# Second attention of a two-block fp32 model: matmuls over the full 128x128 array, other gates, other placing of the projection steps

## The reference

```python
kband, vband = with_prev(kb), with_prev(vb)      # block of 128 tokens and the one before it
s_band = einsum('bnqkgd,bnskd->bnkgqs', qb, kband) * scale + bias_band   # masked to the band
s_meta = einsum('bnqkgd,bmkd->bnkgqm', qb, k_meta) * scale + bias_m      # 16 meta keys
p = softmax(concatenate([s_meta, s_band, sink], -1), -1)
out = einsum(p_meta, v_meta) + einsum(p_band, vband)
y_att = att @ w_attn_branch
merged = sigmoid(g_ssd + gb[0]) * y_ssd + sigmoid(g_att + gb[1]) * y_att
h = h + merged @ w_out
```

## Time and profile before

| | us |
|---|---|
| time, median of 3 runs | 2701.64 (2695.93 to 2713.91) |
| the profiled execution, time | 2691.95 |
| its span, first to last instruction | 2690.0 |
| PE busy in the span | 2522.0 (94%) |
| DVE busy | 1632.3 (61%) |
| ACT busy | 899.1 (33%) |
| mean granted TensorE clock of the span | 0.965 |

### The profile page before, as it was taken

The page is one execution under the profiler, slowest core; times in us unless marked ns, Lnnn a source line. Parts: engine busy times, 40 slices in busy tenths (PEclk is TensorE's granted clock), DMA queues, the critical chain, the costliest instruction groups (busy, mean ns, idle before and its releaser), DMA issues.

```text
span 2690.0 us, 40344 instructions
## 1 busy us (share of the span) xinstructions
PE 2522.0 (94%) x15581; PEld 2210.7 (82%) x15581; DVE 1632.3 (61%) x2776; ACT 899.1 (33%) x1341; POOL 62.2 (2%) x55
## 2 busy tenths in 40 slices
PE   6999999998988999999989899889998999999997
PEld 4887888876887987888888788879777789999997
DVE  6556444456387845444587687877554555884684
ACT  3122222234354532222336634652232233222222
POOL 0000000000021000000000000001000000000000
PEclk9999999999988999999999999989998999999998
DMA  4235222334441012222225223412111112223222
GB/s 139 94 102 124 94 94 94 135 118 121 137 114 41 24 63 83 94 94 94 94 80 126 80 71 108 112 58 90 45 54 50 56 63 95 78 88 117 93 94 95
DMA packets 89708, 242.46 MB, mean 90 GB/s; under 512 B 24870, under 2 KB 56102, under 8 KB 65574
## 3 DMA queue, kind: packets, MB, share of 16 engines
q1 hardware_dynamic: 29056, 198.26, 20.7%
q10 hardware_dynamic: 58744, 36.42, 6.2%
q0 software_dynamic: 1760, 5.77, 1.0%
HBM read 230.50 MB, written 11.14 MB: 90 GB/s over the span
## 4 chain that ended last, share of the span: by engine, by line
PE 48%; DVE 8%; issue 3%; ACT 2%; ACTq 0%; DVEq 0%
PE ps L1151 26%; PE ps L927 13%; PE ps L1239 3%; DVE wlo L1389 1%; PE ps L1327 1%; PE ps L1294 1%; ACT L L776 1%; PE ps L1329 1%; PE ps L1330 1%; PE ps L1310 1%; PE ps L1313 0%; PE ps L1293 0%; ACT whi L506 0%; PE ps L1202 0%; PE ps L1204 0%
## 5 line engine op out<-in xcount | busy, mean ns | idle before, releaser
L506 ACT ACTIVATE whi<-raw 128x2048 fp32r<-128x2048 f32 x187 | 357.6, 1912 | 754.3 <-PE ps L927 501.5
L1151 PE MATMUL ps<-parts,whi 128*128 128x264 f32 x2752 | 488.6, 295 | 5.3 <-issue 4.7
L1389 DVE TENSOR_TENSOR wlo<-raw,whi 128x2048 fp32r<-128x2048 f32 x187 | 427.4, 2286 | 66.6 <-ACT whi L506 65.8
L927 PE MATMUL ps<-parts,whi 128*128 128x512 f32 x1360 | 435.0, 401 | 14.7 <-DVE wlo L1389 9.9
L1151 PEld LDWEIGHTS ps<-parts,whi 128*128 128x128 f32 x2752 | 396.2, 193 | 19.4 <-issue 16.7
L927 PEld LDWEIGHTS ps<-parts,whi 128*128 128x128 f32 x1360 | 259.0, 191 | 80.0 <-DVE wlo L1389 9.3
L927 PE MATMUL ps<-parts,wlo 128*128 128x512 f32 x680 | 271.8, 400 | 0.0
L1151 PE MATMUL ps<-parts,wlo 128*128 128x264 f32 x1200 | 247.4, 288 | 0.0
L927 PE MATMUL ps<-Mhi,whi 128*128 128x512 f32 x512 | 203.2, 397 | 5.1 <-DVE Mlo L1480 5.1
L927 PE MATMUL ps<-Mhi,wlo 128*128 128x512 f32 x512 | 203.0, 396 | 0.0
L927 PE MATMUL ps<-Mlo,whi 128*128 128x512 f32 x512 | 203.0, 396 | 0.0
(11 more groups left out here) (355 smaller groups left out, 4050.4 us busy)
## 6 DMA issues: line engine op xcount, KB each, us to landing
raw<-in_stream SPq DMA_DIRECT2D x187, 1024.0 KB, 4.8
csb<-sums_d ACTq DMA_DIRECT2D x16, 512.0 KB, 5.6
bands<-scratch ACTq DMA_DIRECT2D x6, 1024.0 KB
near<-bands ACTq DMA_DIRECT2D x20, 256.0 KB, 2.6
csf<-sums_d ACTq DMA_DIRECT2D x32, 128.0 KB, 6.0
Qst<-parts POOLq DMA_DIRECT2D x14, 256.0 KB, 6.3
tabs<-bands ACTq DMA_DIRECT2D x8, 418.0 KB, 3.0
...
```

Of the source, the lines that this page charges most:

```text
L506: nc.scalar.activation(whi[:, s, :], raw[:, s, :], ACT.Copy).then_inc(hi_done, 1)
L927: mm = nc.tensor.matmul(out, w[:, s, at], x(k), start=k + j == 0, stop=k == k_tiles - 1 and j == 2)
L1151: mm = nc.tensor.matmul(ps[:, 2 * par + h, 0:HALF], w[:, s, at], x[:, k, h * HALF:(h + 1) * HALF], start=k + j == 0, stop=k == k_tiles - 1 ...
L1389: nc.vector.tensor_tensor(wlo[:, s, :], raw[:, s, :], whi[:, s, :].bitcast(F32), ALU.subtract).then_inc(lo_done, 1)
```

## The change

- Scores: a head's keys are kept in `keys2` with zeros in the other head's 64 rows, so `scores(n)` is one matmul over all 128 rows: 273 columns (previous chunk, sink and meta, own chunk; 145 for the first chunk; 34 for both heads' meta queries in step 8). `Pb` and the bias table are laid out in that order, which cuts one of the DMAs that spread the table (early in the program) in two.
- Values: `vals2` has a zero slot beside each chunk's values, so a slice of 128 weight columns puts the result into the head's half of the partitions and zeros into the other. One matmul per block of keys serves up to 256 queries (its own chunk and the next one); the steps alternate between the heads. `Pb` keeps all eight steps' rows.
- Meta keys: their probabilities of all eight steps are gathered on DVE (`meta_columns`), transposed once and used in four matmuls at the end of the pair (`values_meta`).
- Gates: sigmoid(x) becomes (1 + tanh(x/2))/2. The bias goes into the tanh on ACT, the 1 into the multiply on DVE, the factor 1/2 into the addition after `out`.
- k-steps: the first tile of the loop is done ahead of the pairs; then two k-steps stand in front of each attention step (three ahead of the first; one in the last pair of each `i`, which has one tile less).
- `split_low` is cut into two halves, put behind different steps.

The diff, cut to its core (of the pair loop on PE and on DVE the new lines only; the old ones are in the listing above):

```diff
+                keys2 = sb("keys2", [P, 2, QT, ROW1], F32, scope)
+                vals2 = sb("vals2", [P, 2 * QT + 1, DH], F32, scope)
...
+                Pb = sb("Pb", [P, 2 * QT, ROW], F32, scope)
...
-                    spread(bands2[:, :, ROW0:ROW], two + BAND2 + P - 1, P, 2 * P)
+                    spread(bands2[:, :, 0:P], two + BAND2 + P - 1, P, P)
+                    spread(bands2[:, :, P + ROW0:ROW], two + BAND2 + 2 * P - 1, P, P)
...
-                    act.wait_ge(gs_new, i * 4 + (p + 1))
-                    nc.scalar.activation(sq[:, 0, :], sq[:, 0, :], ACT.Sigmoid).then_inc(gs_sig, 1)
-                    for n in range(8):
-                        if n < 7:
-                            exps(n + 2)
-                        if n == 0 and p % 2 == 0:
+                    for n in range(7):
+                        exps(n + 2)
+                        if n == 2 and p % 2 == 0:
                             next_unit("pair", 3 * p // 2, turn=i * 6, half_turn=i * 3)
+                        if n == 3:
+                            act.wait_ge(mt_free, i * 12 + (T0["pair"] + 3 * p + 2))
+                            nc.scalar.activation(sq[:, 0, :], sq[:, 0, :], ACT.Tanh, scale=0.5, bias=gate_h[:, bass.ds(i * 4 + p, 1)]).then_inc(gs_sig, 1)
...
             with pe.Fori(0, 2) as i:
+                def pair_tile(rr, ks):
+                    tile2("pair", rr // 2, rr % 2, H2, ks, turn=i * 6)
+                pair_tile(0, range(KT))
                 for p in range(4):
                     base = i * 40 + 10 * p
+                    steps = [(3 * p + 1 + j, k) for j in range(3 if p < 3 else 2) for k in range(KT)]
+                    def dense(n):
+                        for _ in range(n):
+                            rr, k = steps.pop(0)
+                            pair_tile(rr, range(k, k + 1))
                     def scores(n):
                         if n >= 2:
+                            pe.wait_ge(ttr2, base + (n - 1))
                         if n == 8:
+                            mm = nc.tensor.matmul(ps[:, 4, 0:2 * ROW0], Q2[:, 0:P], keys2[:, :, 0, 0:ROW0], start=True, stop=True)
                         else:
+                            h, c = n % 2, 1 + n // 2
+                            at = CHUNKS[c][0]
+                            row = keys2[:, h, :, :].rearrange("p c n -> p (c n)")
+                            keys = row[:, (c - 2) * ROW1 + ROW0:c * ROW1] if c > 1 else row[:, 0:ROW1]
+                            mm = nc.tensor.matmul(ps[:, 4 + n % 2, 0 if c > 1 else P:ROW], Q2[:, at:at + P], keys, start=True, stop=True)
+                        mm.then_inc(s2_full, 1)
+                    def turn(n):
+                        pe.wait_ge(p2_ready, i * 36 + (9 * p + n + 1))
+                        if n or p:
+                            pe.wait_ge(pt2_dve, base + n)
+                        if n >= 2:
+                            nc.tensor.transpose(ps[:, 6, 0:P], Pb[:, n, 0:P], ident)
+                        nc.tensor.transpose(ps[:, 6, P:2 * P], Pb[:, n, P + ROW0:ROW], ident).then_inc(pt2_full, 1)
...
+                    def values(n):
+                        pe.wait_ge(pt2_dve, base + (n + 1))
+                        h, c = n % 2, 1 + n // 2
+                        if n == 2 and p:
                             pe.wait_ge(at_ready, i * 4 + p)
+                        for block in range(c - 2, c if c == QT else c - 1):
+                            w = 2 * P if block < QT - 1 else P
+                            mm = nc.tensor.matmul(ps[:, 7, block * P:block * P + w], vals2[:, 2 * block + 1 - h:2 * block + 3 - h, :].rearrange("p a d -> p (a d)"),
+                                                  PT2[:, h, 2 * block * P:2 * block * P + w], start=n == 2, stop=False, skip_group_check=True)
+                    def values_meta():
+                        pe.wait_ge(pt2_dve, base + 10)
+                        for c in range(QT):
+                            mm = nc.tensor.matmul(ps[:, 7, c * P:(c + 1) * P], vmeta[:, c, :], PTm[:, :], start=False, stop=c == QT - 1, skip_group_check=True)
+                        mm.then_inc(o2_full, 1)
...
+                    if not p:
+                        pe.wait_ge(kv_staged, i + 1)
+                    dense(2)
+                    pe.wait_ge(mt_free, i * 12 + (T0["pair"] + 3 * p + 1))
                     if p:
+                        pe.wait_ge(first_done, i * 4 + p)
                     scores(0)
                     scores(1)
                     for n in range(8):
+                        dense(3 if not n else 2 if p < 3 else 1)
                         if n < 7:
                             scores(n + 2)
+                        if n >= 3:
                             values(n - 1)
                         turn(n)
+                    dense(1)
+                    turn_first()
                     values(7)
+                    turn_meta()
+                    dense(2)
+                    values_first()
+                    values_meta()
+                    dense(len(steps))
...
+            own.mark(nc.vector.memset(keys2[:, :, :, :], 0.0))
+            own.mark(nc.vector.memset(vals2[:, :, :], 0.0))
...
+                    nc.vector.scalar_tensor_tensor(halves(Q2[:, :]), product_ready(3 * p), DH ** -0.5, halves(R[:, :]), ALU.mult, ALU.mult).then_inc(mt_free, 1)
                     dve.wait_ge(tabs_loaded, i * 128 + 32 * (p + 1))
                     softmax_in(0)
                     softmax_in(1)
+                    if p:
+                        heads_high(p - 1)
                     for n in range(8):
+                        softmax_out(n)
                         if n < 7:
                             softmax_in(n + 2)
+                        else:
+                            meta_columns()
+                            softmax_out(8)
+                        turned(n)
+                        if n == 0 and p:
+                            heads_low(p - 1)
+                        if n in (1, 2) and p % 2:
+                            split_low("pair", 3 * p // 2, i * 6, n - 1)
+                        if n == 3:
+                            nc.vector.tensor_tensor(halves(sq[:, 0, :]), product_ready(3 * p + 1), halves(R[:, :]), ALU.mult).then_inc(mt_free, 1)
+                        if n in (4, 5) and p % 2 == 0:
+                            split_low("pair", 3 * p // 2, i * 6, n - 4)
+                        if n == 6:
                             dve.wait_ge(gs_sig, i * 4 + (p + 1))
+                            y = t_at(YS, i * 4 + p)
+                            nc.vector.scalar_tensor_tensor(y, sq[:, 0, :], 1.0, y, ALU.add, ALU.mult)
+                        if n == 7 and p < 3:
+                            gate_att()
+                    turned_first()
+                    if p == 1:
+                        split_low("pair", 2, i * 6, 0)
+                    turned_meta()
+                    if p == 1:
+                        split_low("pair", 2, i * 6, 1)
+                    first_out()
+                    if p == 3:
+                        gate_att()
+                        split_low("pair", 5, i * 6)
+                heads_high(3)
+                heads_low(3)
...
-                nc.vector.tensor_tensor(halves(m), product(k % 2), halves(GA[:, k, :]), ALU.mult).then_inc(mt_free, 1)
+                nc.vector.scalar_tensor_tensor(halves(m), halves(GA[:, k, :]), 1.0, product(k % 2), ALU.add, ALU.mult).then_inc(mt_free, 1)
```

250 lines of the change are left out of this document (95 added, 155 removed).

## The result

The changed kernel takes 2627.04 us (median of 4 runs, 2621.43 to 2628.94); the kernel before, on the same chip, 2698.78 us (4 runs, 2690.26 to 2713.91). The ratio is 0.9732 with a 95% interval of [0.9701, 0.9763]: 72 us faster.

The account below looks back on a forecast made before the run. TensorE bounds the loop by its work, its clock and waits for DVE. Pairs 220.4, turn 3.4, slow first tile 8.8, waits 10, low stretches 6 make 248.6 against 307.3; with 1 and 1.8 against it, 56 less: 2646 us, range 2632 to 2660.

Parts of the forecast that it names:

- Matmul prices: Full-array fp32 matmuls in the loop: 0.47 us for 273-column scores, 0.45 for 256-column values, weight loads hidden.
- The rival of exposed loads: Full-array matmuls in the loop expose their weight loads: a pair takes 32.4 us, time 2669 us; chance 20%.
- There are again about 12 breaks, so nothing changes there: K-steps of a pair: about 12 interruptions at 0.20 us more each, 2.4 us, as in the kernel before.
- Waits, 10 us: PE waiting for DVE between attention steps: the old 12.2 us go, 4 to 5 us for each i replace them.
- the rival of DVE late: PE waits some 0.3 us in each of 64 steps, 20 us: 2664 us, or 2687 with high prices; chance 15%.
- Clock: two low stretches, 6 us: Last pair of each i: one 6.8 us stretch at the low clock stays, costing 3.1 us, 6 us for two.
- The loop's turn: Between the two i: PE's 3.4 us wait stays, then a slow first tile of 8.8 us; 1 us added for staging.
- Ahead of the loop: Before the first pair, where PE waits for DVE: new memsets and the product into `PTm` add 1.8 us.
- Free. The extra DMA of the bias table is some 1,000 us early: Early in the program: the additional bias-table DMA costs nothing, since it comes long before its use.
- Gates: In the loop: removing sigmoid table loads from ACT and bias additions from DVE is worth nothing by itself.
- still faster, without new waits and low stretches: Case for the whole kernel: no new PE waits or low-clock stretches in the loop, 2628 us; chance 3%.
- The median of the runs was 10 us above it: Whole kernel: the old median's 10 us above its profiled execution was carried over, taking 2636 to 2646 us.

Follow-up runs that it names:

- s64: The changed kernel with the eight scores matmuls of a pair reading 64 rows instead of 128: 2641.2 us, ratio 0.9775 to the kernel before.
- v64: The changed kernel with the twelve values matmuls of a pair on 64 weight columns instead of 128: 2633.6 us, ratio 0.975 to the kernel before.
- bsplit: The kernel before with only one bias-table DMA of 256 columns split into two of 128: 2715.8 us, ratio 1.004.
- btanh: The kernel before with only the loop gate's sigmoid replaced by a tanh, factors left out: 2707.7 us, ratio 1.0013.
- thin: The changed kernel with one k-step instead of two between steps in pairs 0 to 2: 2640.6 us, ratio 0.9773 to the kernel before.

## Where the prediction was right, and which steps failed

Two steps of the prediction failed above all: the price of a break, which it kept at 0.20 us for a kernel without half-array matmuls, and the 10 us that it added to get from the profiled execution to the median. Waits and low clock were put too high beside them. Of the 19 us between 2646 and 2627, 7 come from the sum of the parts, and 12 from the step from one execution to the median (last in this section).

**Matmul prices: right.** 0.47 and 0.45 us forecast, 0.46 and 0.43 measured. The records start 0.23 apart. The Trainium skill's rule ("TensorE: Matmul & The Clock Gate", section "Packing small matmuls": a weight load overlaps only where the row group differs) does not describe these rows; full-array loads are hidden, and what costs time is next to half-height and half-width ones (s64, v64). The rival of exposed loads is out.

**"There are again about 12 breaks, so nothing changes there": wrong, the largest miss in the loop.** I had measured 0.20 a break between full-array k-steps and half-height matmuls and carried it to a kernel without them. 24 x 0.72 and 9.3 are 26.6, a pair measures 27.15: all breaks cost under 0.6 and not 2.4. With either kind of half-array matmul put back the breaks return: 0.19 around the scores of s64, 0.14 around the values of v64. 29.0 became 27.15, or 14.8 us over the loop.

**Waits, 10 us: 4.6.** The place was right, the last pair of each i (2.0 us, 3.4 forecast) and pair 1 (0.33, 0.6 forecast); the size was twice too large. The stretches last 5.9 us beyond 27.15 a pair, 1.3 more than the recorded waits, so 5.9 stands in the sum below. For the old kernel the prediction counted 4 waits in 64 steps as its reason against the rival of DVE late; the list behind the earlier trace rows has 20.

**Clock: two low stretches, 6 us: none.** I had put them at four waits within 8 us in the last pair. These are there (0.56, 0.80, 0.48, 0.16, within 12.4 us) and the clock stays at 1.00. In the other runs low stretches stand in the steps behind waits of 1.08 to 1.87 us, and not behind each of these (last section).

**The loop's turn: 3.4 + 8.8 + 1 = 13.2 forecast, 15.0 measured.** PE's own wait is 1.9, the first tile 7.6, then 3.5 for the staging, and 2.0 for slow k-steps behind this stall. I had the staging ready "just when PE needs it" at 12.2, and added 1: it was ready at 13.0, which is right. What the sum lacked are the 2.0 us of slow k-steps behind a stall.

**The sum of the loop.** 205.6 for the pairs (27.15 x 8 less two tiles of 5.8), 15.0 and 5.9 make 226.5; measured 226.8, forecast 248.6 + 1.

**Ahead of the loop: 1.8 forecast, 2.9 measured.** The memsets took 1.7 us as reckoned; DVE's staging also ran beside POOL (1.43 and 1.77 us instead of 0.35 and 0.69).

**"Free. The extra DMA of the bias table is some 1,000 us early": wrong.** I asked when its data is needed, and not what its issue holds up. It costs 9 to 10 us (bsplit). This is a miss in the other direction: without it the forecast would have been 9 to 10 us further off, so that it came this near is luck. The other 3 us of the 12.7 lie in the scatter of the nine profiles (1869.0 to 1874.8).

**Gates: nothing, and it was nothing in the old kernel (btanh).** In the new one it was not tried. **Rival of DVE late in every pair:** only when one k-step is left (thin, 14.3 us of waits). The case "still faster, without new waits and low stretches", 2628 us, had 3%; the measured time is there, but with 4.6 us of waits and with cheap breaks, which no case had.

By terms: 14.8 for breaks, 4.1 for waits and 6 for the clock came more, 1.8 at the turn came less (it includes the 1 us); 1.1 ahead of the loop, 12.7 ahead of that, and 2.1 behind it were lost: -56 + (-14.8 - 4.1 - 6 + 1.8) + 1.1 + 12.7 + 2.1 = -63, the distance of the profiles. The terms that came more and those that were lost nearly cancel, 24.9 against 17.7.

**"The median of the runs was 10 us above it": wrong, 12 of the 19 us.** The sum gave 2636 for the profiled execution, and it was 2628.94. To reach the median I added the 10 us by which the kernel before lay above its profiled execution, as if they were a constant. In the changed kernel the median lies 1.9 us below the profiled one. In the kernel before these microseconds go with the granted clock of the execution (0.965 to 0.956 over its 26 runs, 22.4 us); the four runs of the changed kernel have 0.968 to 0.964 and 7.5 us. Without this step the forecast would have been 2636, 9 us above the measured time instead of 19.

## What to carry to other kernels

A matmul on half of the array has two prices: its own, and that of the change of shape on both sides of it. Here that is 0.19 and 0.19 us in each step for the scores, 0.15 and 0.14 for the values; read a break's price from neighbours of the shape that the new kernel will have. A DMA that is needed late is not free when an engine on the path issues it: look at what else is outstanding on that queue. Two k-steps in front of every step cover DVE's chain of 1.5 us and nearly all the rest of its work, one does not. And the distance of a profiled execution from the median belongs to the kernel that was profiled: don't carry it to one whose waits and clock will differ.
